# Reordering DVE and ACT between the last layer norm of a mixer block and the first RMS norm behind it, with two split remainders moved to POOL

## The reference

```
# end of the first block
return layer_norm(ALPHA * x + gate * out, ln_g, ln_b)
# start of each layer of the second block
h = rms_norm(x, norm_mix[l])     # x * rsqrt(mean(x*x) + eps) * gain
proj = h @ w_in[l]               # dq, dk, dv, sq, sk, sv, gates
```

## Time and profile before

| | |
|---|---|
| median of 3 runs | 2186.05 us (2183.84 to 2186.2) |
| the profiled execution, its own time | 2183.68 us |
| its span | 2181.9 us |
| TensorE busy | 2154.6 us (99%) |
| DVE busy | 1257.4 us (58%) |
| ACT busy | 770.6 us (35%) |
| POOL busy | 23.8 us (1%) |
| mean granted TensorE clock | 0.998 |

### The profile page before, as it was taken

How to read it: one execution, slowest core, us unless ns; L and a number is a source line. 1 busy time by engine, 2 the same in 40 slices (tenths; PEclk the granted TensorE clock), 3 DMA queues, 4 the chain that set the end, 5 groups by cost and what they waited for, 6 DMA issues and landing times.

```text
span 2181.9 us, 25074 instructions
## 1 busy us (share of the span) xinstructions
PE 2154.6 (99%) x10451; PEld 1780.0 (82%) x10451; DVE 1257.4 (58%) x1617; ACT 770.6 (35%) x1019; POOL 23.8 (1%) x40
## 2 busy tenths in 40 slices
PE   6999999999999999999999999999999999999998
PEld 3888888888888888888888888888888888888887
DVE  7899797944665847434765554234743476555422
ACT  2323232223343354344353333135434435333311
POOL 1000000000000100000000000000000000000000
PEclk9999999999999999999999999999999999999999
DMA  9432332232232222322223233222232222323322
GB/s 319 139 116 83 97 101 83 97 116 97 97 102 97 97 81 76 115 77 78 97 77 106 88 107 106 87 76 92 77 115 77 77 97 78 104 89 107 106 88 77
DMA packets 180788, 217.87 MB, mean 100 GB/s; under 512 B 3772, under 2 KB 152900, under 8 KB 180420
## 3 DMA queue, kind: packets, MB, share of 16 engines
q1 hardware_dynamic: 178000, 210.52, 29.1%
q10 hardware_dynamic: 2228, 3.60, 0.5%
q0 software_dynamic: 448, 2.15, 0.2%
HBM read 212.06 MB, written 4.19 MB: 99 GB/s over the span
## 4 chain that ended last, share of the span: by engine, by line
PE 95%; DVE 1%; SPq 1%; ACT 1%; DMA 1%; issue 1%; POOL 0%; POOLq 0%; ACTq 0%; DVEq 0%
PE psum L1692 30%; PE psum L1693 30%; PE psum L1694 30%; PE psum L2033 1%; SPq L617 1%; PE psum L2064 1%; PE psum L2096 1%; DMA raw<-in_w_in 1%; PE psum L2076 1%; PE psum L2020 0%; PE psum L2049 0%; DVE whl L503 0%; PE psum L1716 0%; ACT hT L832 0%; DVE hT L1393 0%
## 5 line engine op out<-in xcount | busy, mean ns | idle before, releaser
L1692 PE MATMUL psum<-hT,whl 128*128 128x512 f32 (+1 forms) x2080 | 796.5, 383 | 2.9 <-DVE hT L1117 1.9
L1693 PE MATMUL psum<-hT,whl 128*128 128x512 f32 (+1 forms) x2080 | 790.2, 380 | 0.0
L1694 PE MATMUL psum<-hT,whl 128*128 128x512 f32 (+1 forms) x2080 | 790.2, 380 | 0.0
L503 DVE TENSOR_TENSOR whl<-raw,whl 128x1024 fp32r<-128x1024 f32 (+1 forms) x364 | 441.7, 1216 | 457.0 <-ACT whl L496 456.7
L496 ACT ACTIVATE whl<-raw 128x1024 fp32r<-128x1024 f32 (+1 forms) x364 | 379.6, 1047 | 448.1 <-PE psum L1694 420.2
L1692 PEld LDWEIGHTS psum<-hT,whl 128*128 128x128 f32 x2080 | 391.7, 188 | 84.6 <-issue 5.7
L1694 PEld LDWEIGHTS psum<-hT,whl 128*128 128x128 f32 x2080 | 391.8, 188 | 74.4
L1693 PEld LDWEIGHTS psum<-hT,whl 128*128 128x128 f32 x2080 | 391.9, 188 | 72.6 <-issue 0.5
L1692 PE MATMUL psum<-whl,ff 128*128 128x512 f32 x352 | 137.1, 390 | 0.0
L1694 PE MATMUL psum<-whl,ff 128*128 128x512 f32 x352 | 137.0, 389 | 0.0
L1693 PE MATMUL psum<-whl,ff 128*128 128x512 f32 x352 | 137.0, 389 | 0.0
(11 more groups left out here) (285 smaller groups left out, 2114.9 us busy)
## 6 DMA issues: line engine op xcount, KB each, us to landing
raw<-in_w_in SPq DMA_DIRECT2D x88, 1024.0 KB, 5.1
raw<-in_w_up SPq DMA_DIRECT2D x44, 1024.0 KB, 5.1
raw<-in_w_down SPq DMA_DIRECT2D x20, 1024.0 KB, 5.0
ada<-in_w_ada SPq DMA_DIRECT2D x12, 1024.0 KB, 13.7
raw<-in_w_branch SPq DMA_DIRECT2D x12, 1024.0 KB, 4.9
raw<-in_w_out SPq DMA_DIRECT2D x12, 1024.0 KB, 5.0
x<-in_x SPq DMA_DIRECT2D x4, 512.0 KB, 6.2
v_by_token<-vnat ACTq DMA_DIRECT2D x4, 512.0 KB, 3.0
```

The source lines that it names most:

```text
L503: nc.vector.tensor_tensor(whl_view(w, 1), raw_view(w), whl_view(w, 0).bitcast(F), ALU.subtract).then_inc(w_lo, 1)
L1692: M(out_, stat_hi, mov_hi, start=start, stop=False, **kw)
L1693: M(out_, stat_hi, mov_lo, start=False, stop=False, **kw)
L1694: return M(out_, stat_lo, mov_hi, start=False, stop=stop, **kw)
```

## The change

On DVE, the mean squares of token blocks 0 to 2 no longer stand inside `first_rows(1, tb + 1)` but one place earlier, behind or in front of `first_rows(0, ...)`. `gained(2, 0)` moves in front of `first_rows(0, 2)`, and `gained(2, 1)` with `norm_lo(2, 1)` in front of `first_rows(0, 3)`. The remainders of pieces w0 + 6 and w0 + 7 leave DVE. POOL computes them, with the same subtraction, right behind the roots (2, 2) and (1, 3). DVE gets a wait on `w_lo` in front of the next remainder that it makes itself. On ACT, `scaled(2, 2)` moves in front of the split of piece w0 + 7.

```diff
@@ POOL's program
             for i_, (s, tb) in enumerate(ORDER):
                 pool.wait_ge(s_ms, i_ + 1)
                 nc.gpsimd.tensor_tensor(rstd[:, tb:tb + 1], msq[:, tb:tb + 1], neghalf[:, 0:1], ALU.pow).then_inc(s_rstd, 1)
+                if (s, tb) in ((2, 2), (1, 3)):
+                    w = resident(ROWS[0]) + (6 if s == 2 else 7)
+                    pool.wait_ge(w_lo, w)
+                    pool.wait_ge(w_hi, w + 1)
+                    nc.gpsimd.tensor_tensor(whl_view(w, 1), raw_view(w), whl_view(w, 0).bitcast(F), ALU.subtract).then_inc(w_lo, 1)
@@ ACT's norm(s) for s == 2
                     split_hi(w0 + 6)
                     norm_sum(s, 2)
                     norm_hi(s, 1)
+                    scaled(s, 2)
                     split_hi(w0 + 7)
-                    scaled(s, 2)
                     norm_sum(s, 3)
@@ DVE's first_rows
-            def first_rows(half, tb, before=None):
+            def first_rows(half, tb):
...
                 if half:
-                    stats = chain[0]
-                    if before is not None:
-                        mean_square(2, before)
-                    dve.wait_ge(dve_chain, stats)
+                    dve.wait_ge(dve_chain, chain[0])
                     row_stats(tb)
@@ DVE's order
             first_rows(0, 1)
-            first_rows(1, 1, 0)
+            mean_square(2, 0)
+            first_rows(1, 1)
             first_normed(1)
+            gained(2, 0)
             first_rows(0, 2)
-            gained(2, 0)
+            mean_square(2, 1)
             norm_lo(2, 0)
-            first_rows(1, 2, 1)
+            first_rows(1, 2)
             first_normed(2)
             split_lo(w0 + 4)
+            gained(2, 1)
             split_lo(w0 + 5)
+            norm_lo(2, 1)
             first_rows(0, 3)
-            split_lo(w0 + 6)
-            gained(2, 1)
-            norm_lo(2, 1)
-            first_rows(1, 3, 2)
-            split_lo(w0 + 7)
+            mean_square(2, 2)
+            first_rows(1, 3)
             first_normed(3)
             gained(2, 2)
             mean_square(2, 3)
@@ DVE, layer l
                 for key in (("sv", l, 1), ("sq", l, 0), ("sq", l, 1), ("sk", l, 0), ("sk", l, 1)):
+                    if key == ("sv", 0, 1):
+                        dve.wait_ge(w_lo, W[key] + 3)
                     split_lo(W[key] + 3)
```

## The result

The changed kernel takes 2188.47 us in the median (2186.48 to 2189.06, 20 runs), the kernel before 2185.89 us (2183.1 to 2186.42, 20 runs). The ratio is 1.0015, with a 95% interval of 1.0009 to 1.0021: some 3.3 us slower (2.0 to 4.6). That is less than the 0.2% that I had called the limit, but its interval is clear of no change. The forecast was 2186.5 us, in a range of 2181.6 to 2189.9. The runs of both kernels fall into two groups, before into 9 near 2183.8 and 11 near 2186.1 us, after into 5 near 2186.7 and 15 near 2188.6; from group to like group the change costs 2.5 to 2.9 us, and the rest of the 3.3 is that more runs lie in the upper one.

What follows compares the result with a forecast made beforehand. TensorE, busy 99%, bounds the kernel, with 2.19 us of waits to win at the border. Four outcomes (-0.7 to +1.8 us) gave +0.5 on 2183.68, so 2184.2; the runs' median lies 2.4 higher: 2186.5 us, range 2181.6 to 2189.9.

Steps and rivals of the forecast that it cites:

- the limit: Whole kernel: 0.2% (4.4 us) taken as about what a measurement can tell from no change.
- the wait before block 3: TensorE before block 3's transposes, border into first attention layer: 1.40 us before, forecast to grow to 2 to 4 us.
- The bound and the ceiling: TensorE busy 99%; its two waits at the border, 0.79 + 1.40 = 2.19 us, are the most any repair gives.
- The rescheduled DVE work: DVE at the border: reordering and one split_lo fewer start first_rows(1, 3) at 756.77 instead of 759.03.
- T: Duration of one 128x1024 subtraction on POOL: taken as 2.4 us, between bounds of 1.21 and 4.5 us.
- The two ties: Whether POOL's subtraction or DVE starts first: first against line 1407, second against line 1422, both after root (1, 3).
- four outcomes: Start of block 3's transposes by who wins: 767.8, 768.7, 769.3 or 770.3, against 768.44; middle +0.6 us.
- Behind block 3 nothing new is late: After block 3's transposes: norm_lo(2, 3) ends 4.71 us after they start, value_rows(3) needs it 6.7 us after.
- Rival 2: Border: no exclusion when POOL is the one that runs; gain 2.2 us, 2183.9 us; chance 0.15.
- Rival 3: Border: slow POOL subtraction, over 3.7 or 4.9 us by who wins; kernel over 0.2% slower; chance 0.08.
- Rival 4: DVE's early order loses its cover: gained(2, 0) delays first_rows(1, 2); costs up to 1 us, 2187; chance 0.03.
- the cover: DVE slack after norm_lo(2, 0), at about 743.8, until bank 5 is full at 744.68: about 0.9 us.

Runs made afterwards that it cites:

- one_each: Changed kernel, but DVE makes the first query remainder and POOL only the second, behind root (2, 3); 2183.09 us, ratio 0.9991 to the kernel before.
- idle_two: both_on_dve plus, on POOL behind the changed kernel's two roots, a same-size subtraction of two rows nobody needs; 2189.42 us, ratio 1.0020 to before.
- idle_none: idle_two with a memset of the 128x1024 tile in place of POOL's subtraction, so POOL only writes; 2183.76 us, ratio 0.9996 to before.
- idle_one: idle_two with POOL multiplying one row by a constant, reading one tile, in place of the subtraction; 2186.4 us, ratio 1.0008 to before.
- dve_late: both_on_dve plus two extra DVE products in front of first_rows(1, 3) and two in front of first_normed(3); 2190.68 us, ratio 1.0026 to before.
- order_only: Changed kernel's new order, but DVE makes both query remainders and POOL does only roots; 2183.54 us, ratio 0.9992 to the kernel before.
- both_on_dve: order_only with the second query remainder on DVE moved behind norm_lo(2, 2); 2183.35 us, ratio 0.9992 to the kernel before.
- halves: Changed kernel with each of POOL's two subtractions cut into two of 512 columns, one waiting for the other; 2185.07 us, ratio 1.0003 to before.
- dve_late_once: both_on_dve plus one extra DVE product, in front of first_normed(3) only; 2185.77 us, ratio 1.0004 to the kernel before.
- second_late: Changed kernel with POOL's second subtraction behind root (2, 3) instead of root (1, 3); 2185.64 us, ratio 1.0003 to the kernel before.
- pool_only: Kernel before with the two query remainders moved from DVE to POOL and nothing else moved; 2189.69 us, ratio 1.0024 to before.

## Why the prediction was right, and where it was off

The time lies in the range, but that says little. The range is 8.3 us wide and would have held no change as well. The forecast put +0.5 us on the kernel before; measured are 2.5 to 2.9 us between like groups of runs and 3.3 by the ratio. The absolute figure owes something to luck too: the same kernel before had a median of 2185.89 us beside the changed one, and of 2184.0 to 2184.1 in the three later rounds (27 to 33 runs each). What holds is the mechanism of the wait before block 3; the clock behind it was missing.

- *The bound and the ceiling* held nearly. With POOL taken out, the new order gives 1.7 us (between 3.5 gained and 0.2 lost), where I had called 2.19 the most. The traces put the ceiling a little higher: one_each is 1.8 us shorter in the border with 0.58 us of wait left.
- *The rescheduled DVE work* held closely. first_rows(1, 3) was to start at 756.77; it starts at 755.80, which is 756.83 on the clock of the trace before. The wait before block 2 is gone, as said.
- *T* was taken as 2.4 us from two bounds a factor of 3.7 apart and measured 2.42 and 2.40; that the middle of such bounds came out to 0.02 us was luck. The Trainium skill's figure ("GPSIMD Engine Reference", section "Elementwise — side-by-side cycle accounting"), by which I had estimated 2.25, was 0.15 to 0.17 short. The Trainium skill's rule of two SBUF inputs ("SBUF — State Buffer", section "Who interferes with whom") holds in both directions here: idle_two shows DVE shut out, idle_none shows that a POOL instruction that only writes shuts out nothing. That it holds for the whole instruction shows in the subtractions, but not in idle_one, where DVE lost 0.87 and 0.78 us to POOL instructions of 2.79 and 3.37 us, part of which may be POOL's own waiting.
- *The two ties.* I had spread the forecast over four outcomes, -0.7 to +1.8 us. Both went to POOL. For that outcome the working gave transposes of block 3 at 765.5 + 2 x 2.41 = 770.3; measured is 768.98 + 1.03 = 770.0, so +1.57 where I had +1.8 (770.3 - 768.44 is 1.9; the least of the four, written -0.7, is 767.8 - 768.44 = -0.6). By putting +0.5 I chose near the middle of the four. Root (2, 3) was to start where the second subtraction ends; that was so in none of the runs with POOL first, since it waited for DVE's mean (764.58 against 767.11). The rows could have told more: POOL's root at 735.19, 0.55 us long, was followed by the next at 735.70, before the first had ended, while DVE started line 1422 only 0.03 us after the root that it waits for. Wherever a whole subtraction on POOL and such a DVE instruction started within 0.1 us of each other, POOL was first (five times in four kernels).
- *The step that failed* is "Behind block 3 nothing new is late". Nothing was late, but TensorE was slow: the wait of 4.1 us was followed by 5 us at the 1.2 GHz level, worth 2.38 us. I had read the granted clock of 1.00 beside waits of 0.79 and 1.40 us, and forecast a wait of 2 to 4 us in one piece without asking what the clock does then. dve_late shows that it belongs to TensorE's wait, however it comes about, and not to POOL. With it the sum is 1.57 + 2.38 = 3.95 us in this pair of traces, with the dip near 1045 left out, against 2.5 to 2.9 us between like groups of runs. The two do not agree closer than that: there is one trace of each kernel, and the time at low clock can differ between executions of one kernel (the granted clock is 0.997 in the five lower runs of the changed kernel and 0.996 in the fifteen upper ones).
- *Rival 2* (no exclusion, -2.2 us) is refuted by the changed kernel's own rows and by idle_two. *Rival 3* (a slow subtraction) is refuted by T. *Rival 4* is refuted by the trace: behind norm_lo(2, 0) DVE idled 0.99 us until bank 5 was full, so the cover I had put at 0.9 us was there.

Counted from the end of w_out to 60 us behind it, and against the trace before, one_each is 1.8 us shorter, order_only, both_on_dve and idle_none 1.3, and halves 0.7; dve_late_once, second_late and idle_one are 1.1 to 1.2 us longer, the changed kernel 3.9, pool_only 4.2, idle_two 4.6 and dve_late 5.2. The clock fell in all those that are longer and in none that is shorter.

What stays open is what decides whether the clock falls. In the traces it fell behind waits of 1.59, 1.96, 1.98, 3.41, 3.78, 4.03 and 4.10 us, and did not behind 0.58, 1.24, 1.40 and 1.85 us. The length of the wait alone is therefore not the rule. Nor is it settled by the kernel: second_late has two runs of eleven at a granted clock of 0.998 and nine at 0.997 or less, and the kernel before has 0.998 in its lower group of runs and 0.996 in nearly all of its upper one, of which there is no trace. So its clock may have fallen in the border too, behind the 1.40 us. Open too are the dips near 1045 and 1750 us, each worth some 1.5 us.

## What to carry to other kernels

An engine that looks idle is not free: before work moves to POOL, look which DVE instructions stand beside it with two inputs in SBUF, and put the POOL instruction where the one that it will shut out is waited for by nobody, or cut it into pieces that DVE can get in between. Where a POOL instruction stands right behind the one that releases a DVE instruction, count on POOL being first. And do not sum TensorE's waits as if they were exchangeable: a long one can cost more than its length, through the clock behind it.

## What the runs showed of the hardware that I had not expected

- A root of 0.55 us beside a long DVE instruction with two SBUF inputs ends about 0.4 us behind it. A DVE instruction shut out by POOL's subtraction ends its own length behind POOL's end, less 0.14 to 0.20 us: 758.90 + 0.69 - 0.14 = 759.45 for line 1412, and 764.58 + 1.28 - 0.20 = 765.66 for line 1424.
- POOL's cost for 128x1024 is 2.36 to 2.42 us with two inputs against 1.22 on DVE, and 0.95 us for a memset.
- TensorE's clock fell to half behind a wait of 1.96 us (second_late), and behind one of 1.59 us with another of 0.35 us close by (dve_late_once), in the midst of a span in which TensorE is 99% busy, and once stayed at 1.00 behind one of 1.85 us (halves). It also fell near 1045 us, where TensorE shows no wait at all (busy 10.00 of 10.00 us, mean clock 0.83).
